# A three-layer fp32 block: later key blocks of stick-breaking tails summed on VectorE, masks merged, and a new order at the start and around one gate piece

## The reference, cut to what matters

```python
mod = c_act @ w_ada[layer] + b_ada[layer]                 # 1 x 3072
shift, scale, gate = jnp.split(mod, 3, axis=-1)
h = rms_norm(x, norm_in_gain[layer]) * (1.0 + scale[:, None, :]) + shift[:, None, :]
proj = h @ w_in[layer]

# stick_breaking_attention, per block of 128 queries, 16 heads of 64
z = jnp.einsum("bqhd,bkhd->bhqk", q[:, start:end], k[:, :end]).astype(jnp.float32) * scale
mask = s_idx < t_idx
log_beta = jax.nn.log_sigmoid(z)
log_one_minus = jnp.where(mask, jax.nn.log_sigmoid(-z), 0.0)
tail = lax.cumsum(log_one_minus, axis=3, reverse=True) - log_one_minus
weights = jnp.exp(jnp.where(mask, log_beta + tail, -jnp.inf))
outs.append(jnp.einsum("bhqk,bkhd->bqhd", weights.astype(v.dtype), v[:, :end]))
```

## Time and profile before

| | |
|---|---|
| median of 3 runs | 1816.65 us (1815.67 to 1817.2) |
| profiled execution | 1815.44 us |
| its span, first to last instruction | 1813.7 us |
| TensorE busy | 1780.4 us, mean granted clock 0.995 |
| VectorE, ScalarE, GpSimd busy | 872.1, 757.8, 646.4 us |

### The profile page before, as it was taken

The page is one execution under the profiler, slowest core; times in us unless marked ns, Lnnn a source line. Parts: engine busy times, 40 slices in busy tenths (PEclk is TensorE's granted clock), DMA queues, the critical chain, the costliest instruction groups (busy, mean ns, idle before and its releaser), DMA issues.

```text
span 1813.7 us, 22075 instructions
## 1 busy us (share of the span) xinstructions
PE 1780.4 (98%) x8677; PEld 1427.4 (79%) x8677; DVE 872.1 (48%) x1301; ACT 757.8 (42%) x1243; POOL 646.4 (36%) x257
## 2 busy tenths in 40 slices
PE   7999999999999999999999999999999999999998
PEld 4887777778887767866988888888876798888886
DVE  6510366664877357944453333335457253333334
ACT  3323555456335253345532322226677352223322
POOL 1443222232335233433444444443410354444442
PEclk9999999999999999999999999999999999999999
DMA  7523322221122322311233222232220222332222
GB/s 289 212 93 116 91 61 59 72 68 48 47 105 89 128 66 67 112 47 51 79 98 109 95 93 93 93 104 73 89 68 1 93 94 93 98 108 95 93 93 82
DMA packets 83906, 166.06 MB, mean 92 GB/s; under 512 B 6026, under 2 KB 8207, under 8 KB 83823
## 3 DMA queue, kind: packets, MB, share of 16 engines
q1 hardware_dynamic: 83822, 164.93, 27.7%
HBM read 157.64 MB, written 2.10 MB: 88 GB/s over the span
## 4 chain that ended last, share of the span: by engine, by line
PE 75%; issue 16%; POOL 4%; DVE 3%; ACT 1%; DMA 0%; POOLq 0%; SPq 0%; DVEq 0%; ACTq 0%
PE PDT L683 12%; PE PDT L685 12%; PE PDT L684 12%; PE PDT L694 8%; PE PDT L696 8%; PE PDT L695 8%; POOL wlo L1985 4%; PE PM L1285 2%; PE PDT L1246 2%; PE PM L1246 1%; PE PM L1225 1%; PE PDT L824 1%; PE PDT L829 1%; PE PDT L823 1%; PE PM L1157 1%
## 5 line engine op out<-in xcount | busy, mean ns | idle before, releaser
L1985 POOL TENSOR_TENSOR wlo<-wraw,whi 128x2048 fp32r<-128x2048 f32 (+5 forms) x172 | 604.0, 3523 | 1019.8 <-ACT whi L1445 981.1
L1445 ACT ACTIVATE whi<-wraw 128x2048 fp32r<-128x2048 f32 (+2 forms) x131 | 244.0, 1863 | 520.2 <-PE PDT L685 303.5
L694 PE MATMUL PDT<-hhi,whi 128*128 128x512 f32 x800 | 314.7, 393 | 0.8 <-POOL wlo L1985 0.8
L695 PE MATMUL PDT<-hlo,whi 128*128 128x512 f32 x800 | 311.5, 389 | 0.0
L696 PE MATMUL PDT<-hhi,wlo 128*128 128x512 f32 x800 | 311.5, 389 | 0.0
L683 PE MATMUL PDT<-whi,hhi 128*128 128x512 f32 (+1 forms) x592 | 234.2, 396 | 0.4 <-POOL wlo L1985 0.4
L685 PE MATMUL PDT<-whi,hlo 128*128 128x512 f32 (+1 forms) x592 | 227.8, 385 | 0.0
L684 PE MATMUL PDT<-wlo,hhi 128*128 128x512 f32 (+1 forms) x592 | 227.8, 385 | 0.0
L683 PE MATMUL PDT<-whi,mh_hi 128*128 128x512 f32 x512 | 199.3, 389 | 0.0
L684 PE MATMUL PDT<-wlo,mh_hi 128*128 128x512 f32 x512 | 199.2, 389 | 0.0
L685 PE MATMUL PDT<-whi,mh_lo 128*128 128x512 f32 x512 | 199.2, 389 | 0.0
(11 more groups left out here) (368 smaller groups left out, 2447.6 us busy)
## 6 DMA issues: line engine op xcount, KB each, us to landing
wraw<-in_mlp_w SPq DMA_DIRECT2D x64, 1024.0 KB, 5.2
wraw<-in_w_in SPq DMA_DIRECT2D x26, 1024.0 KB, 5.0
wraw<-in_even_w_in SPq DMA_DIRECT2D x16, 1024.0 KB, 5.2
w_ada<-in_w_ada SPq DMA_DIRECT2D x12, 1024.0 KB, 12.9
wraw<-in_w_out SPq DMA_DIRECT2D x8, 1024.0 KB, 5.1
swapped<-qk_sb SPq DMA_DIRECT2D x16, 256.0 KB, 6.8
wraw<-in_even_w_out SPq DMA_DIRECT2D x4, 1024.0 KB, 5.0
wraw<-in_odd_w_o SPq DMA_DIRECT2D x4, 1024.0 KB, 5.0
```

The costliest lines, as they stand in the source:

```text
L694: mm(bank, sth, hi[:, k0 + k, :], start=start and k == 0, stop=False)
L695: mm(bank, sth, lo[:, k0 + k, :], start=False, stop=False)
L1445: nc.scalar.activation(whi[base % 2][:, 0:n], wraw[base % 2][:, 0:n], ACT.Copy).then_inc(S("w_hi"), 1)
L1985: part = g.tensor_tensor(wlo[base % 2][:, cols], wraw[base % 2][:, cols], fl(whi[base % 2][:, cols]), ALU.subtract)
```

## The change

The tails: VectorE adds the later key blocks' l for each query block (`later_sums`: one 256-column sum, which gives blocks 1+2 for query block 2 and 2+3 for query block 3, and one 128-column sum, which gives 1+2+3), so each key block needs one product with minus ones over `SB_LATER`'s columns. `sb_l` grows from 1280 to 1664 columns, the sums lying in it between the banks' shares; `sb_lo` lies in the same place as `sb_l`. The middle chunk of the high and low halves is 640 columns wide instead of 256 and waits for the sums. The tails of bank 0 start on the first chunk and wait for the second before their minus ones. The two masks of bank 0 become one product.

The start: load 3 comes in two halves with semaphores of their own; TensorE's rows are added into row 0 of `acc` on VectorE, and one-column products with ones then add over partitions and turn in one (`fold`), which replaces `total`, the copies and `columns`. The first products go tile by tile over four banks, high halves of h first. VectorE makes the first `wlo` after sum 4, before sums 5 and 7.

The second attention: the last gate piece is cut in four parts of three products: before the wait for the last transposed tile, after the logits of head 1, and after the turnings of heads 0 and 1. ScalarE copies its bank in head 2.

```diff
-    sb_l = arena("sb_l", [P, 1280], 48)
-    sb_hi = arena("sb_hi", [P, 1280], 53, F32R)
-    sb_lo = arena("sb_lo", [P, 1280], 58, F32R)
+    sb_l = arena("sb_l", [P, 1664], 48)
+    sb_lo = arena("sb_lo", [P, 1664], 48, F32R)
+    sb_hi = arena("sb_hi", [P, 1664], 54.5, F32R)
...
+    SB_LN = [0, 640, 1152]
+    SB_SPLIT = [(0, 512), (512, 1152), (1152, 1664)]
+    SB_SUM02, SB_SUM13, SB_SUM03 = 512, 896, 1024
+    SB_LATER = {2: (384, 1, 128), 1: (640, 2, 256), 0: (0, 3, 512)}
...
-        for n in range(4):
+        for n in range(3):
             ada(n)
+        for part, sem in enumerate(("ada_part", "ada_loaded3")):
+            load(wview(ADA_SLOTS[3], 4, 512)[:, 2 * part:2 * part + 2, :],
+                 w_ada_v[:, 4 + 2 * part:6 + 2 * part, ADA_COLUMNS[1]:ADA_COLUMNS[1] + 512], sem)
...
-        def total(chunk, bank, fresh, made):
+        def fold(chunk, made):
 
             pe.wait_ge(S("dve_pieces"), made)
-            mm(PM[:, bank, :], ones[:, :], acc[chunk][:, :], start=fresh, stop=True).then_inc(S("mod_sum"), 1)
-
-        def columns(half):
...
+            for j in range(4):
+                c0 = 4 * (chunk % 2) + j
+                last = mm(PM[:, 2 - chunk // 2 * 2, c0:c0 + 1], acc[chunk][:, j * P:j * P + P], ones[:, 0:1],
+                          start=c0 == 0, stop=True, skip_group_check=True)
             last.then_inc(S("mod_sum"), 1)
...
-            for f in range(4):
-                for k in range(4):
...
+            for k in range(4):
+                pe.wait_ge(S("h_hi"), 4 * h + k + 1)
+                for f in range(4):
+                    mm(PD[f], wh[:, k, f * P:f * P + P], hhi[:, 4 * h + k, :], start=h == 0 and k == 0, stop=False)
+                pe.wait_ge(S("h_made"), 4 * h + k + 1)
+                for f in range(4):
+                    mm(PD[f], wh[:, k, f * P:f * P + P], hlo[:, 4 * h + k, :], start=False, stop=False)
             if h == 0:
-                total(2, 2, True, 4)
-                total(3, 3, False, 5)
+                weigh(6, 3)
             unit_wait(h)
...
             if h == 0:
                 last.then_inc(S("w_used"), 1)
+                fold(2, 4)
+                fold(3, 5)
...
             for n, blocks in enumerate(SB_CHUNKS):
+                o, mask = PM[:, n, 0:P], mask_t[:, :]
+                if len(blocks) == 2:
+                    o = PM[:, n, :].rearrange("p (a b) -> p a b", b=P)[:, 0:4:3, :]
+                    mask = mask_t[:, :].unsqueeze(1).to_broadcast([P, 2, P])
+                last = mm(o, identr[:, :], mask, start=False, stop=False, skip_group_check=True)
+                last.then_inc(S("sb_z"), 1)
+
+        def sb_tails(h):
+
+            def tail(n, c0, w, ones_or_triangle, columns, last):
+                o = PM[:, n, c0:c0 + w]
+                for part in (sb_hi, sb_lo):
+                    first, count, step = columns
+                    moving = part[:, first:first + w]
+                    if count > 1 and step > P:
+                        moving = part[:, first:first + count * step].rearrange("p (a b) -> p a b", a=count)[:, :, 0:P]
+                        o = PM[:, n, c0:c0 + w].rearrange("p (a b) -> p a b", a=count)
+                    op = mm(o, ones_or_triangle[:, :], moving, start=False, stop=last and part is sb_lo,
+                            skip_group_check=True)
+                return op
+
+            for n, blocks in enumerate(SB_CHUNKS):
+                pe.wait_ge(S("sb_split"), 3 * h + (1, 2, 3)[n])
                 for s, c0 in blocks:
...
+                    first = SB_LN[n] + c0
+                    last = tail(n, c0, SEQ - s * P, neg_ge, (first, 1, P), False)
+                if n == 0:
+                    pe.wait_ge(S("sb_split"), 3 * h + 2)
+                s, c0 = blocks[0]
+                last = tail(n, c0 + P, SEQ - s * P - P, neg_one, SB_LATER[s], True)
                 last.then_inc(S("sb_tail"), 1)
...
+        def gate_part(k):
+
+            name, r, h, b = GATE_PIECES[7]
+            u = PH[name][0] + 2 * r + h
+            unit_wait(u)
+            wh, wl = wview(whi[u % 2], 4, 512), wview(wlo[u % 2], 4, 512)
+            mm(PD[b], wh[:, k, b * P:b * P + P], hhi[:, 4 + k, :], start=False, stop=False)
+            mm(PD[b], wh[:, k, b * P:b * P + P], hlo[:, 4 + k, :], start=False, stop=False)
+            last = mm(PD[b], wl[:, k, b * P:b * P + P], hhi[:, 4 + k, :], start=False, stop=k == 3)
+            if k == 3:
+                full(last, b)
...
+        gate_part(0)
         transposed("qk", 8)
...
             if h == 1:
-                piece(*GATE_PIECES[7])
+                gate_part(1)
             if 1 <= h <= A_H:
                 turn_probs(h - 1, pr)
+            if h in (1, 2):
+                gate_part(h + 1)
...
-                a = slice(SB_FIRST[n], SB_FIRST[n] + SB_WIDE[n])
-                act.wait_ge(S("sb_softplus"), 3 * h + n + 1)
+                a = slice(*SB_SPLIT[n])
+                act.wait_ge(S("sb_softplus"), 4 * h + (1, 3, 4)[n])
                 nc.scalar.activation(sb_hi[:, a], sb_l[:, a], ACT.Copy).then_inc(S("sb_high"), 1)
...
-            if h == 1:
-                after_piece(*GATE_PIECES[7])
             if 1 <= h <= A_H:
                 turned(h - 1, prt)
             if h < A_H:
                 exps(h, pr, mx, den, ((2, 0), (3, 1)))
+            if h == 2:
+                after_piece(*GATE_PIECES[7])
...
+            if row is not None:
+                bank, taken = row
+                link(op)
+                dve.wait_ge(S("pe_pieces"), taken)
+                op = v.tensor_tensor(a[0:1, :], a[0:1, :], PM[0:1, bank, :], ALU.add)
             op.then_inc(S("dve_pieces"), 1)
...
-        weigh(1, True)
-        weigh(3, True)
+        weigh(1, True, (0, 1))
+        weigh(3, True, (1, 2))
         modulation(0)
         weigh(4, True)
+        dve.wait_ge(S("w_hi"), 1)
+        v.tensor_tensor(wlo[0][:, :], wraw[0][:, :], fl(whi[0][:, :]), ALU.subtract).then_inc(S("w_split"), 1)
         dve.wait_ge(S("dve_pieces"), 3)
         weigh(5, False)
-        weigh(7, True)
-        dve.wait_ge(S("w_hi"), 1)
-        v.tensor_tensor(wlo[0][:, :], wraw[0][:, :], fl(whi[0][:, :]), ALU.subtract).then_inc(S("w_split"), 1)
+        weigh(7, True, (3, 3))
         modulation(1)
...
+        def later_sums(h):
+
+            def two(first, step):
+                return sb_l[:, first:first + 2 * step].rearrange("p (a b) -> p a b", a=2)[:, :, 0:P]
+
+            dve.wait_ge(S("sb_softplus"), 4 * h + 2)
+            link(v.tensor_tensor(two(SB_SUM02, SB_SUM13 - SB_SUM02), two(SB_LN[1], P), two(P, 2 * P), ALU.add))
+            v.tensor_tensor(sb_l[:, SB_SUM03:SB_SUM03 + P], sb_l[:, 2 * P:3 * P], sb_l[:, SB_SUM13:SB_SUM13 + P],
+                            ALU.add).then_inc(S("sb_softplus"), 1)
...
                 v.tensor_tensor(sb_l[:, a], PM[:, n, 0:SB_WIDE[n]], sb_l[:, a], ALU.max).then_inc(S("sb_softplus"), 1)
+                if n == 1:
+                    later_sums(h)
             for n in range(3):
-                a = slice(SB_FIRST[n], SB_FIRST[n] + SB_WIDE[n])
+                a = slice(*SB_SPLIT[n])
+                dve.wait_ge(S("sb_softplus"), 4 * h + (3, 3, 4)[n])
                 dve.wait_ge(S("sb_high"), 3 * h + n + 1)
                 v.tensor_tensor(sb_lo[:, a], sb_l[:, a], fl(sb_hi[:, a]), ALU.subtract).then_inc(S("sb_split"), 1)
```

More of the change, by code:

```diff
@@ L926, in weigh @@
             for k in range(4):
-                last = mm(PM[:, bank, :], silu_w[:, 4 * (n % 2) + k, :], w[:, k, :], start=k == 0, stop=False)
+                last = mm(PM[:, bank, :], silu_w[:, 4 * (n % 2) + k, :], w[:, k, :], start=k == 0, stop=k == 3)
             last.then_inc(S("pe_pieces"), 1)
-        def total(chunk, bank, fresh, made):
+        def fold(chunk, made):
             pe.wait_ge(S("dve_pieces"), made)
-            mm(PM[:, bank, :], ones[:, :], acc[chunk][:, :], start=fresh, stop=True).then_inc(S("mod_sum"), 1)
-        def columns(half):
[L937 to L942, removed]
+            for j in range(4):
+                c0 = 4 * (chunk % 2) + j
+                last = mm(PM[:, 2 - chunk // 2 * 2, c0:c0 + 1], acc[chunk][:, j * P:j * P + P], ones[:, 0:1],
+                          start=c0 == 0, stop=True, skip_group_check=True)
             last.then_inc(S("mod_sum"), 1)
@@ L949, in _ @@
         weigh(2, 1)
-        total(0, 0, False, 1)
-        total(1, 1, False, 2)
-        columns(0)
+        fold(0, 1)
+        fold(1, 2)
         def first_half(h):
@@ L1020, in sb_scores @@
             for n, blocks in enumerate(SB_CHUNKS):
-                for s, c0 in blocks:
-                    last = mm(PM[:, n, c0:c0 + P], identr[:, :], mask_t[:, :], start=False, stop=False,
-                              skip_group_check=True)
+                o, mask = PM[:, n, 0:P], mask_t[:, :]
+                if len(blocks) == 2:
+                    o = PM[:, n, :].rearrange("p (a b) -> p a b", b=P)[:, 0:4:3, :]
```

(12 more changed lines are left out.)

31 lines of the change are left out of this document (6 added, 25 removed).

## The result

The changed kernel takes **1805.56 us** (median of 4 runs, 1804.74 to 1807.02) against 1816.93 us for the kernel before in the same session (4 runs): ratio 0.9941, 95% interval 0.9928 to 0.9953. That is 11 us faster, where 20.7 were predicted, and just outside the range. The span of the profiled execution fell from 1813.7 to 1803.0 us.

The account below looks back on a forecast made before the run. TensorE, busy 98% of the span, was taken as the bound. Terms 10.7 + 1.7 + 1.0 + 0.3 + 4.0 + 3.0 = 20.7 us off 1815.44 gave 1794.7, predicted as a 1796 us median; range 1791 to 1804.

Parts of the forecast that it names:

- Tails: Attention loop: 14 products instead of 20 per head, 2.05 us instead of 2.72, saving 10.7 us over 16 heads.
- Slower than before: Rival, loop: stepped moving operands run at the plain fp32 pace, 29 us lost in all, 1825 us; chance 0.03.
- Masks: Attention loop: four 128-wide mask products become one of 256 and two of 128, saving 0.10 us a head, 1.7 in all.
- The longer VectorE chain: Loop: VectorE's added sums fit its idle time and low halves arrive in time; gain 1.0 us, plus 0.3 in head 0.
- Every one of these meets its user within 0.1 us: Loop, odd heads: low halves are ready about when TensorE needs them, so 0.6 us of loss was kept over seven heads.
- The VectorE rival: Loop: sums or 640-wide halves come late and TensorE waits in eight uncovered heads, 5.3 us less gain, 1801 us; chance 0.14.
- The start: Start of the kernel, up to the third weight unit: its first product at 58.4 us instead of 62.42, 4.0 us gained.
- (b): Start: first products tile by tile, first low half before VectorE's later sums; second half's first tile at 45.7 instead of 51.26.
- The gate piece: Second attention: splitting the last gate piece fills TensorE's gaps and mostly avoids a half-clock stretch, 3.0 us of 0 to 3.8.
- The chain's part: Second attention: turning starts at 797.6 instead of 799.7, logits of head 2 at 800.0 instead of 802.13, 2.1 us.
- The sign named for it: Second attention: no stretch at half clock after the logits of head 3 would show the split gate piece working.
- two rivals together: Range's slow end: late VectorE in the loop plus little from start and gate, total gain 7.6 us, 1804 us.

Follow-up runs that it names:

- experiment 4: Three kernels leaving nothing out: the changed kernel with four GpSimd loop subtractions retimed, head 13's given to VectorE, and three different starts; 1796.98, 1795.42, 1792.99 us.
- the second version of experiment 4: The changed kernel with four GpSimd loop subtractions retimed, head 13's given to VectorE, and GpSimd's second-unit subtraction at the start made later: 1795.42 us, ratio 0.9875.
- experiment 1: GpSimd's loop subtractions cut to 64 columns, for timing only: in the changed kernel 1798.7 us (0.9905), in the kernel before 1814.73 us (0.9993).
- the best version: The changed kernel with GpSimd's loop subtractions retimed, head 13's given to VectorE, and the second weight unit's low part made by VectorE: 1792.99 us, ratio 0.9864.

## Why the prediction was wrong, point by point

- **Tails** (2.05 us, 10.7 in all): right. 2.08 or 2.09 in even heads (2.18 and 2.19 in heads 10 and 6, behind a hold), 2.20 to 2.22 in undisturbed odd ones, where 2.1 to 2.2 had been named. Its two terms are off against each other: the four 128-column products take 0.34 us, not 0.44, the ten wider ones 1.75, not 1.61. Slower than before through stepped operands: no sign of it.
- **Masks** (0.10 us a head): right as a price, 0.50 to 0.39 or 0.40 us, by other parts (0.22 and 0.17 us, where 0.12 and 0.22 had been put). The Trainium skill (SBUF — State Buffer, Door 1) has non-contiguous PSUM access slow matmuls significantly; here the trace disagrees: the merged product, in two runs of 128 columns, keeps the queue 0.22 us where a single one of 128 in its place takes 0.16, so the added run costs 0.06, the pace of the tails. In the changed kernel only 0.84 of the 1.7 us reached the loop's length.
- **The longer VectorE chain:** right where it was priced. The sums cost 0.42 and 0.29 us (0.40 and 0.28 forecast), the 640-wide low half arrives, and the pieces of the undisturbed odd heads fell from 5.66 to 5.53 us (those of all seven in experiment 4). The step that failed is the sentence "Every one of these meets its user within 0.1 us": it took VectorE's durations from one undisturbed head and asked which engines feed it, not what GpSimd does beside it. With less margin left, a hold delays the tails by what sticks out of it: 4.2 us of holding in head 7 cost 1.7. Against the second version of experiment 4, heads 7 and 11 lose 1.53 us before their tails and 0.14 in them, head 15 loses 1.36, head 0 0.6, and head 13 2.15: 3.35 + 1.35 + 0.6 + 2.15 = 7.45 us, which is 263.79 - 256.33. Head 13 is not a hold: there TensorE itself waits for GpSimd's low part, a path that the prediction did not name. About 0.95 us of it is head 13's wait, which the kernel before had as well; so without these delays the change gives 14.1 - 0.95 = 13.1 us of the 13.7 predicted.
- **The VectorE rival** came near in size (5.3 us less in uncovered heads, 7.1 were missing in the loop) with the wrong cause: experiment 1 shows that VectorE's own chain is in time.
- **The start** (4.0 us): the step that failed is (b), "The first low half of the weights now comes before VectorE's later sums". The move was costed on VectorE alone. GpSimd's subtraction of the second unit waits for VectorE's of the first, so it moved too, from 42.95, behind the sums, to 38.55, onto the last of them, one step of which took 4.96 us in place of about 0.75. The first half went as worked out (low products end at 42.19, forecast 42.5); the second began at 48.75, not 45.7. With that meeting removed, and the low part made by VectorE, it begins at 45.24 and the third unit at 58.99: 3.4 us of the 4.0. This stretch scatters by some 2 us from profile to profile, so the 0.4 of the one pair is no sharp number.
- **The gate piece** (3.0 us): 3.6 in this pair. The chain's part, put at 2.1, is 365.26 - 363.2 = 2.1 against the profile whose clock stayed up; the remaining 1.6 is the clock, put at 0.9. The sign named for it held: the granted clock stays at 1.00 from 796 to 820 us.
- **The range** held two rivals together, both of other mechanisms; that one mechanism could take both terms at once was not in it. By place the best version saves 3.4 + 14.0 + 3.6 = 21.0 us of span.

The rule that I had at hand and did not weigh is in the Trainium skill, SBUF — State Buffer, Who interferes with whom: VectorE and GpSimd share one pair of SBUF ports as an exclusive lock, and a VectorE operation with two SBUF inputs contends with a GpSimd one that reads SBUF. The trace agrees: 4.95 us instead of 0.75, its end 0.55 us behind GpSimd's, and the instructions with an input in PSUM free. The same section of the Trainium skill counts tensor_scalar among the operations that can enter a mode which takes the shared ports, and the trace shows it held from SBUF to SBUF (4.81 us instead of 0.54). That the ports are the cause is the Trainium skill's word; the runs show the holding and its removal.

## What to carry to other kernels

When an instruction is moved or a slack used up, look at the engine beside it, not only at the ones that feed it: what else does the moved step release, and does it now run beside a VectorE instruction on the path? What a hold costs is not its length but what of it sticks out past the slack behind it. A group whose mean is far above its median, here 926 ns against 752 in the kernel before, already shows that such meetings happen (there a single one of 24 was held). Adding a wait to the second engine only helps if it ends past every such instruction and still ahead of its own user; giving the work to VectorE, when it has 2.3 us free, can be better (1795.4 to 1793.0 us here). And a wait of TensorE of 1.5 to 2 us can cost as much again in clock, or nothing, so read the clock behind it before you count a gain that came back as lost.

## What was not expected of the hardware

- A held instruction need not be a long one: a 128x4 one took 2.63 us instead of 0.16, to the end of GpSimd's subtraction. Nor is every instruction that reads SBUF held: later in the changed kernel a MAX8 over 512 columns kept its 0.68 us in the middle of one (at 701.35). And the one that starts first is not held: a VectorE step of 0.75 us kept its time when GpSimd began 0.05 us behind it, and GpSimd's subtraction took 5.14 us instead of the usual 4.6.
- Behind the same wait of 1.9 us the granted clock was 1.00 in one profile and 0.50 in another, a difference of 1.5 us for the next piece. What decides it stays open.
- The start of the same code scatters by 1.8 us between profiles (62.42 to 64.17 for the third unit in four of them). Its cause was not sought.
